# A row of scales spread by TensorE instead of a transfer, and a re-ordered, merged routing step in a three-mixer transformer kernel

## The reference

```
def pool_mixer(h, w, scale):          # first mixer, on h = rms_norm(x, norm_mix[0])
    ...                                # windowed means over 2, 4, 8, 16 tokens, minus h itself
    y = jnp.einsum('bsgc,gcd->bsgd', p, w).reshape(B, S, D)
    return y * scale                   # a row of 1024 numbers

def hier_moe(x, w_group, b_group, w_router, b_router, w_gate, w_up, w_down):
    logit_g = (xt @ w_group + b_group).astype(F32)         # 4 groups
    g_sel = jnp.argmax(logit_g, -1)
    logit_e = (xt @ w_router + b_router).astype(F32).reshape(n_tok, N_GROUPS, EXPERTS_PER_GROUP)
    logit_e = jnp.take_along_axis(logit_e, g_sel[:, None, None], 1)[:, 0]
    top_v, top_i = lax.top_k(jax.nn.softmax(logit_e, -1), TOP_K_IN_GROUP)   # 2 of the group's 4
    ...                                # y += combine * ((silu(x wg) * (x wu)) wd), for each expert
```

## Time and profile before

| | |
|---|---|
| median of 3 runs | 1508.41 us (1507.11 to 1509.01) |
| the profiled execution | 1508.41 us, of it 1503.0 us span of the instructions |
| TensorE busy | 1473.0 us, 98% of the span |
| VectorE, ScalarE, GpSimd busy | 1023.8, 796.3 and 408.6 us |
| transfers | 226.27 MB, mean 151 GB/s |
| granted TensorE clock | 0.994 of full speed over the span |

### The profile page before, as it was taken

The page is one execution under the profiler, slowest core; times in us unless marked ns, Lnnn a source line. Parts: engine busy times, 40 slices in busy tenths (PEclk is TensorE's granted clock), DMA queues, the critical chain, the costliest instruction groups (busy, mean ns, idle before and its releaser), DMA issues.

```text
span 1503.0 us, 23779 instructions
## 1 busy us (share of the span) xinstructions
PE 1473.0 (98%) x8733; PEld 1276.9 (85%) x8733; DVE 1023.8 (68%) x1277; ACT 796.3 (53%) x1224; POOL 408.6 (27%) x253
## 2 busy tenths in 40 slices
PE   9999999999999999999999999999989999999996
PEld 8999999788987789999998888888668888888875
DVE  7499999442675335899995236336784699988885
ACT  6445565232455424555554235443773477787774
POOL 0567777000000003688771000000130011222111
PEclk9999999999999999999999999999999899999999
DMA  6222333323230022222333322322006499999994
GB/s 253 85 82 85 112 105 104 128 84 116 87 121 1 32 95 88 81 87 108 112 112 113 112 98 85 129 85 85 29 1 264 161 339 393 394 393 394 384 374 114
DMA packets 36215, 226.27 MB, mean 151 GB/s; under 512 B 5271, under 2 KB 5527, under 8 KB 11824
## 3 DMA queue, kind: packets, MB, share of 16 engines
q1 hardware_dynamic: 31392, 212.06, 37.8%
q0 software_dynamic: 4608, 13.22, 3.8%
q10 hardware_dynamic: 144, 0.03, 0.0%
HBM read 215.22 MB, written 13.63 MB: 152 GB/s over the span
## 4 chain that ended last, share of the span: by engine, by line
PE 57%; DMA 3%; DVE 3%; ACT 1%; issue 1%; POOLq 0%; DVEq 0%; ACTq 0%; SPq 0%
PE PS L269 17%; PE PS L271 17%; PE PS L270 17%; DMA eraw<-experts 3%; PE PS L2084 1%; PE PS L2814 1%; PE PS L2095 1%; PE PS L2104 1%; PE PS L2459 0%; PE PS L1865 0%; PE PS L310 0%; ACT WEH L2885 0%; DVE da_flat L2194 0%; PE PS L2837 0%; DMA out<-X,expert_index 0%
## 5 line engine op out<-in xcount | busy, mean ns | idle before, releaser
L264 DVE TENSOR_TENSOR WL<-raw,WH 128x2048 fp32r<-128x2048 f32 x53 | 124.6, 2351 | 228.1 <-ACT WH L259 227.9
L2948 DVE TENSOR_TENSOR WEL<-eraw,WEH 128x2048 fp32r<-128x2048 f32 x96 | 217.6, 2286 | 21.4 <-ACT WEH L2885 21.4
L259 ACT ACTIVATE WH<-raw 128x2048 fp32r<-128x2048 f32 x51 | 97.7, 1915 | 229.0 <-PE PS L271 229.0
L2885 ACT ACTIVATE WEH<-eraw 128x2048 fp32r<-128x2048 f32 x96 | 182.3, 1914 | 33.9 <-DMA eraw<-experts 22.6
L269 PE MATMUL PS<-AH,WL 128*128 128x256 f32 (+1 forms) x624 | 185.4, 297 | 0.9 <-DVE WL L929 0.3
L271 PE MATMUL PS<-AH,WH 128*128 128x256 f32 (+1 forms) x624 | 183.5, 294 | 0.0
L270 PE MATMUL PS<-AL,WH 128*128 128x256 f32 (+1 forms) x624 | 183.3, 294 | 0.0
L929 DVE TENSOR_TENSOR WL<-plain,WH 128x512 fp32r<-128x512 f32 x136 | 153.0, 1125 | 21.4 <-ACT WH L816 19.9
L269 PE MATMUL PS<-WH,AL 128*128 128x512 f32 (+2 forms) x416 | 155.0, 373 | 1.6 <-DVE AL L2295 1.3
L271 PE MATMUL PS<-WH,AH 128*128 128x512 f32 (+2 forms) x416 | 152.7, 367 | 0.0
L270 PE MATMUL PS<-WL,AH 128*128 128x512 f32 (+2 forms) x416 | 152.5, 367 | 0.0
(11 more groups left out here) (385 smaller groups left out, 3758.2 us busy)
## 6 DMA issues: line engine op xcount, KB each, us to landing
eraw<-experts SPq DMA_DIRECT2D x96, 1024.0 KB, 16.1
raw<-stream SPq DMA_DIRECT2D x94, 1024.0 KB, 4.8
out<-X SPq DMA_DIRECT2D x5, 512.0 KB, 3.5
moe_rows<-moe_rows_g SPq DMA_DIRECT2D x5, 512.0 KB, 3.1
X<-x SPq DMA_DIRECT2D x4, 512.0 KB, 6.1
ffn_row<-rows SPq DMA_DIRECT2D x2, 512.0 KB, 9.9
final_row<-rows SPq DMA_DIRECT2D x2, 512.0 KB, 6.1
cst<-consts SPq DMA_DIRECT2D x1, 739.5 KB, 13.6
```

The source lines that it names most:

```text
L259: act.activation(WH[:, u % SLOTS, :], raw[:, u % SLOTS, :], ACT.Copy).then_inc(unit_hi, 1)
L264: dve.tensor_tensor(WL[:, u % SLOTS, :], raw[:, u % SLOTS, :], WH[:, u % SLOTS, :].bitcast(F32), ALU.subtract).then_inc(unit_lo, 1)
L2885: act.activation(WEH[:, k % ESLOTS, :], eraw[:, k % ERAW, :], ACT.Copy).then_inc(unit_hi, 1)
L2948: dve.tensor_tensor(WEL[:, k % ESLOTS, :], eraw[:, k % ERAW, :], WEH[:, k % ESLOTS, :].bitcast(F32), ALU.subtract).then_inc(unit_lo, 1)
```

## The change

Three places are edited.

At the start, the broadcast transfer of the scale row is dropped from SyncE's list. One row of 1024 numbers (4 KB) is loaded by ScalarE's queue ahead of the gains, TensorE multiplies a column of ones by it into PSUM banks 6 and 7, after pooling tile 0 and ahead of tile 1, and VectorE's multiplication of unit 0 reads it from there. Banks 6 and 7 are those of tile 3, so TensorE waits for that multiplication (`w_scaled`) ahead of pooling tile 3.

In `route`, TensorE issues two `keep_busy` matmuls on weights between the two halves of the last tile's transposes, where the first half of tile 2's logits stood, and all 16 remaining logit matmuls follow the second half. VectorE's `select` first makes a tile that tells where a group is the best (`group`), and then handles two token tiles by one instruction: 1 + 1 + 2 instructions instead of 2 + 4. The index for the first round is now a copy of the first part of `slot_index`, made after it.

In `run_experts`, GpSimd waits for the index once, ahead of the four first gathers, and does one increment of a semaphore less.

```
-                    scale_row = sb("pool_scale_row", [P, D], where=early)
+                    scale_row = sb("pool_scale_row", [1, D], where=early)
...
-                    sp.dma_start(scale_row[:, :], rows[0:1, :].broadcast_to([P, D])).then_inc(row_here, 16)
...
+                    act.dma_start(scale_row[:, :], rows[0:1, :]).then_inc(row_here, 16)
                     act.dma_start(gain[:, :], gains[:, :]).then_inc(gains_here, 16)
...
-                    dve.wait_ge(row_here, 16)
+                    dve.wait_ge(row_spread, 1)
                     w4 = raw[:, 0, :].rearrange("p (g k d) -> p g k d", g=4, k=2)
-                    dve.tensor_tensor(w4, w4, scale_row[:, :].rearrange("p (g d) -> p g d", g=4).unsqueeze(2)
+                    dve.tensor_tensor(w4, w4, PS[:, 6:8, :].rearrange("p a (g d) -> p (a g) d", g=2).unsqueeze(2)
                                       .broadcast_to([P, 4, 2, 256]), ALU.mult).then_inc(w_scaled, 1)
...
                     for t in range(T):
+                        if t == 1:
+                            pe.wait_ge(row_here, 16)
+                            for side in range(2):
+                                mm = pe.matmul(PS[:, 6 + side, :], warm[0:1, 0:P].bitcast(F32),
+                                               scale_row[:, side * 512:side * 512 + 512], start=True, stop=True)
+                            mm.then_inc(row_spread, 1)
+                        if t == T - 1:
+                            pe.wait_ge(w_scaled, 1)
...
                 turn_x(last, 0)
-                logits(2, 0)
+                keep_busy(pe, 0, 2, WH[:, (u0 + 3) % SLOTS, :])
                 turn_x(last, 1)
-                logits(2, 1)
-                logits(last, 0)
-                logits(last, 1)
+                for t in (2, last):
+                    logits(t, 0)
+                    logits(t, 1)
...
-                    for t in (2 * pair, 2 * pair + 1):
-                        ins = ranked_as(m.both[:, t, :], t, 1.5, ALU.is_lt)
-                    ins.then_inc(selected, 1)
+                    then(dve.tensor_scalar(m.group[:, ts, :], m.rank[:, ts, 0, :], 0.0, None, ALU.is_equal))
+                    group = m.group[:, ts, :].unsqueeze(3).broadcast_to([P, 2, G, 4])
+                    dve.scalar_tensor_tensor(m.both[:, ts, :].rearrange("p t (g e) -> p t g e", g=G), m.rank[:, ts, 1:5, :],
+                                             1.5, group, ALU.is_lt, ALU.mult).then_inc(selected, 1)
                     for k in range(2):
-                        for t in (2 * pair, 2 * pair + 1):
-                            ins = ranked_as(m.chosen[:, k, t, :], t, float(k), ALU.is_equal)
+                        ins = dve.scalar_tensor_tensor(m.chosen[:, k, ts, :].rearrange("p t (g e) -> p t g e", g=G),
+                                                       m.rank[:, ts, 1:5, :], float(k), group, ALU.is_equal, ALU.mult)
...
-                dve.scalar_tensor_tensor(m.index[:, :], PS[:, 3, 0:E], -1.0, m.nothing[:, 0:E], ALU.add,
-                                         ALU.add).then_inc(index_ready, 1)
-                dve.scalar_tensor_tensor(m.slot_index[:, 0:ROUNDS, :].rearrange("p r e -> p (r e)"),
-                                         PS[:, 3, 0:ROUNDS * E], -1.0, m.nothing[:, :], ALU.add, ALU.add)
+                then(dve.scalar_tensor_tensor(m.slot_index[:, 0:ROUNDS, :].rearrange("p r e -> p (r e)"),
+                                              PS[:, 3, 0:ROUNDS * E], -1.0, m.nothing[:, :], ALU.add, ALU.add))
+                dve.tensor_copy(m.index[:, :], m.slot_index[:, 0, :]).then_inc(index_ready, 1)
...
-                        if n == 0:
-                            pool.wait_ge(index_ready, r + 1)
-                            pool.sem_inc(gather_allowed, 1)
...
+                    pool.wait_ge(index_ready, r + 1)
                     for n in range(4):
                         gather(n)
```

More of the change, by code:

```diff
@@ L336, in through_latent_attention @@
             row_here = sem("pool_row_here")
+            row_spread = sem("pool_row_spread")
             ffn_row_here = sem("ffn_row_here")
@@ L2320, in expert_memory @@
             m.rank = early("route_rank", [P, T, 5, 4])
+            m.group = early("route_group", [P, T, G])
             m.chosen = early("route_chosen", [P, 2, T, E])
```

## The result

The changed kernel took **1516.43 us** (median of 20 runs, 1503.57 to 1521.57), the kernel before on the same chip 1507.21 (20 runs, 1505.15 to 1509.27): a ratio of **1.0051**, 95% interval 1.0036 to 1.0065. I had forecast 1509.9, in 1507.9 to 1511.9. The profiled execution took 1516.76 us, with a span of 1515.0. One thing is needed to read these numbers: the executions of the changed kernel are of two kinds, four of the twenty at 1503.6 to 1506.2 and sixteen at 1515.2 to 1521.6, with none between (of all 53 executions, seven at 1502.5 to 1506.2 and 46 at 1514.5 to 1521.6). The ratio takes in both kinds and lies near that of the means, 1.0049; that of the two medians is 1.0061.

What follows compares the result with a forecast made beforehand. TensorE was taken as the bound, busy 1473.0 of 1503.0 us. From 1508.41, start +1.4 and routing +0.1 (order 0, select +0.1, index 0) gave 1509.9 us, range 1507.9 to 1511.9.

Steps and rivals of the forecast that it cites:

- Matmuls added: Start: two float32 matmuls of 512 columns between tiles 0 and 1 take 1.82 us, bounds 1.13 and 3.6.
- slower by more than a measurement can tell: Rival, 7%: clock falls behind the one-row matmuls at the start, pooling runs at half speed; 1511.6 to 1515, say 1513.
- The lower bound of that term: Start: the two added matmuls take at most 1.13 us, as L2084 with 64 rows; start then about +0.65.
- tile 0's addition: Start: VectorE adds tile 0's product 1.36 us later, and everything after is later by that; start +1.4.
- Second transposes: Routing: start at about 1182.82 instead of 1183.07, after VectorE's addition ending at 1182.76; 0.25 earlier.
- TensorE's order: Routing: two fillers add 0.5 us, paid by transposes 0.25 earlier and by the clock; net 0.
- the clock falls inside the logits: Rival, 20%: routing clock falls as before, 8 to 9 logit records left, ended 0.9 us later; 1510.8.
- Select: Routing: VectorE's select takes 0.4 instead of 0.26, ranking released 0.15 later; +0.1, between 0 and +0.2.
- Index: Routing: index 0.2 later, at 1194.1, hidden since GpSimd is past its waits only at 1194.36; 0, between -0.1 and +0.2.
- TensorE has no gap of size until the attentions: After the start: nothing later gives the start's delay back, so shifting TensorE's stream costs its full shift.
- one of my signs of being wrong: Routing: GpSimd waiting for the index was listed among the observations that would show the forecast wrong.
- The clock kept through the ranking: Rival, 17%: full clock through the routing's ranking matmuls, VectorE bound by its own work; 0.4 less, 1509.5.

Runs made afterwards that it cites:

- e4: Kernel before plus two unread one-row float32 matmuls of 512 columns between pooling tile 0 and tile 1: 1514.95 us, ratio 1.0045.
- e5: Kernel before plus two unread float32 matmuls of 512 columns over all 128 rows between pooling tile 0 and tile 1: 1502.87 us, ratio 0.9967.
- e8: Kernel before plus two unread float32 matmuls of 512 columns over 64 rows between pooling tile 0 and tile 1: 1504.70 us, ratio 0.9976.
- e2: Kernel before with only the start edits, routing as before: 1515.29 us, ratio 1.0035; its profiled execution kept the clock.
- e9: Kernel before with the start of the change, its scale row zero-padded and spread over 128 rows, and the old routing: 1503.56 us, ratio 0.9974.
- e3: Changed kernel, routing edits included, with the scale row zero-padded to 128 partitions and spread by matmuls over 128 rows: 1506.11 us, ratio 0.9987.
- e1: Kernel before with only the routing edits, start as before: 1508.71 us, ratio 1.0011.
- e12: Changed kernel with its spread in two parts, one one-row matmul ahead of tile 1, one ahead of tile 2: 1512.77 us, ratio 1.0026.
- e10: Kernel before plus eight TensorE instructions (two unread float32 matmuls of 16 columns) in the routing, at about 1187 us: 1504.04 us, ratio 0.9974.

## Why the prediction was wrong

**The failed step** is the one under "Matmuls added": "I take 1.82, since both matmuls use the same row of the array." As a duration it was right, 12.38 - 10.47 = 1.91. As the whole cost it was wrong. The sum took the clock behind them for full, and the rival that did not, "slower by more than a measurement can tell", got 7%. Its mechanism is what happened: the clock falls behind the one-row matmuls and the pooling runs at half speed. I held against it that the pair streams 1024 columns. e4 and e5 show that it streams just as many with 128 rows and that at this length the rows decide. The lower bound of that term was wrong as well: it came from L2084, with 64 rows and 1.13 us, but e8's pair with 64 rows takes 1.91, as one row does. I had the earlier trace rows, a stretch that is 100% busy and yet loses the clock, and drew from it only for the routing.

**The rival's price was short as well.** I took the 10 us of the routing's fall for its length, and then mostly a third of it: at most 5 us lost. It lasted 20.48 us here and 23.9 in e4. From 12.38 to tile 0's addition it cost 11.8 - 2.4 = 9.4 us.

**The start without the fall.** Forecast +1.36 at tile 0's addition; e2 has +1.09 and e5 +1.12. Tile 3 was squared at 12.50, forecast 12.7; the low part of unit 0 ended at 16.77 + 3.24 = 20.01, forecast 19.5 to 20; TensorE never waited for `w_scaled` ahead of tile 3. The chain was right, the clock under it was not. In after's own execution another 0.9 us had gone before the edit, since the clock rose at 6.77 and not at 4.69 us; it rises anywhere between 4.4 and 7.4 in the profiled executions, whichever the kernel. At half speed that is worth up to 1.5 of the 4.1 us by which the twenty executions of before differ.

**The routing.** Second transposes: forecast 1.00 after the first, measured 1.01 (1193.22 and 1194.23). TensorE's order: forecast 0, measured +0.46 in after (from the first transposes to the last logit's reader, 1193.22 to 1198.68 against 1181.82 to 1186.82), +0.7 between e9 and e3. The forecast paid for the fillers' 0.5 us with the 0.46 that before loses by its clock inside the logits; after lost it there too, in part. (That step's 0.23 us for one filler should read 0.25, as its own row gives; its sum has 0.5 for two and does not change.) I had 32 records at 0.106, 3.40; they took 3.69, since the clock fell at 1198.02, before the last of them:

```profile
1194.23 0.66 PE L2460 MATMUL PS<-cst,X 128*128 128x128 f32 x4
1194.72 3.85 PE L2469 MATMUL PS<-router_weights,moe_turned 128*128 128x20 f32 x32
1198.41 1.04 PE L2478 MATMUL PS<-route_told,AL 128*128 128x64 f32 x4
```

So it lay between my forecast and "the clock falls inside the logits". Select: forecast +0.15 on VectorE, measured `both` complete at 1200.23 + 0.19 = 1200.42, 0.39 after the first of the two instructions, against 0.26, +0.13. Index: forecast +0.2; the copy ends 0.43 after the first of the two instructions starts, against 0.17, so +0.26. As a sum it came out as forecast: the index came 12.2 us later than before, but the gather only 11.9 (1207.17 against 1195.24). The reason was another, and one of my signs of being wrong: GpSimd now waits for the index. The chain of waits in after:

```profile
1205.96 0.18 DVE expert_index L2734
1206.15 0.03 issue
1206.18 0.05 POOLq L3020
...
1206.29 0.65 issue
```

From the index to the 0.65 us ahead of the gather it is 1206.29 - 1206.13 = 0.16 us, before 1194.36 - 1193.88 = 0.48. The shorter way behind the wait, and not slack ahead of it, pays for the later index. Together the routing is +0.4 in after by the distance from its first transposes (11.4) to what follows the gather (11.8), where I had +0.1. e3 against e9 has 1.2, and e1's ratio of 1.0011, 0.2 to 3.0 us, allows either. The clock kept through the ranking did not occur.

**What no step spoke of.** The eight instructions added at the start move the 16 KB pieces of TensorE's code: -1.7 us at the loop's exit and -3.6 outside the span. Both stalls were in the profile of before, the first as a wait "issue" of 1.55 us, the second as a time 5.4 us longer than the span, and I had read neither. I wrote that "TensorE has no gap of size until the attentions". It has, at 265.7 us.

**The sum after the fact,** for the two profiled executions, with each term read from the distances above and not measured by itself: the clock's later rise +0.9, the spread +1.5, the fall +9.4, code -1.7 and -3.6, the stretch with the short fall +1.2, routing +0.4: +8.1, measured +8.35.

## What to carry over

A matmul over few rows is not priced by its duration alone. Where it runs for a microsecond or two, ask what the clock does behind it, and where the row is there anyway, zero-pad it to more partitions: 64 rows were enough here. And before a kernel is called tuned, compare its time with its span and look for waits ended by "issue": a few instructions more or less in front of them can be worth more than the edit itself, in either direction, so an edit that adds or drops TensorE instructions has to be tested against an empty one of the same count.

## What the hardware showed that I had not expected

- A pair of one-row float32 matmuls, 1.9 us, took the clock to half for 20 to 24 us of uninterrupted TensorE work; with 64 or 128 rows (e8, e5, e3, e9: 39 executions, none above 1509) it never did; with one row and 16 columns, about 0.5 us, it did not either (8 executions). In the changed kernel 16 of 20 timed executions fell, with its start alone 9 of 12, in the split one 8 of 12, so it is near an edge that I cannot place. The profiled executions that fell had their clock rise at 6.77 and 5.66 us (after, e4), those that kept it at 4.39 and 5.12 (e2, e12); whether the moment of that rise decides was not tested.
- Eight unread instructions made a kernel 4.4 us faster (1503.59 against 1507.97).
- A 16 KB piece that came late at a loop's exit went with a TensorE wait of 1.55 to 2.00 us (before, e10, e1), and the absence of one behind the end with mostly 1.8 (at most 3.3) instead of 3.8 to 5.8 us outside the span. That the pieces hold TensorE's code, and that they are what is waited for, is inferred.
- Left open: the short falls of 3.4 us at varying places (268.6, 1126.8, 1136.6), and what sets the moment of the clock's rise.
